# A GpSimd low part behind six norms, and the norm's inverse and spread ahead of the barrier

## The reference, cut to what matters

```
def rms_norm(x, g):
    xf = xf * lax.rsqrt(jnp.mean(xf * xf, axis=-1, keepdims=True) + RMS_EPS)
    return (xf * g.astype(jnp.float32)).astype(x.dtype)

h = modulate(rms_norm(x, norm_g[l, 1]), shift[:, 1], scale[:, 1])
x = x + gate[:, 1, None, :] * token_mixer(h, ...)
```

## Time and profile before

| what | value |
| --- | --- |
| median of 3 runs | 2968.79 us (2968.53 to 2969.40) |
| profiled execution, time | 2971.32 us |
| profiled execution, span | 2969.4 us |
| mean granted TensorE clock | 0.976 of full |
| TensorE matmul / weight load busy | 2870.5 (97%) / 2664.5 (90%) us |
| VectorE / ScalarE / GpSimd busy | 2183.7 (74%) / 1369.5 (46%) / 178.3 (6%) us |
| chain that ended last | TensorE 66%, VectorE 8%, weight load 4%, ScalarE 1% of the span |

### The profile page before, as it was taken

How to read it: one execution, slowest core, us unless ns; L and a number is a source line. 1 busy time by engine, 2 the same in 40 slices (tenths; PEclk the granted TensorE clock), 3 DMA queues, 4 the chain that set the end, 5 groups by cost and what they waited for, 6 DMA issues and landing times.

```text
span 2969.4 us, 61005 instructions
## 1 busy us (share of the span) xinstructions
PE 2870.5 (97%) x22452; PEld 2664.5 (90%) x22452; DVE 2183.7 (74%) x3774; ACT 1369.5 (46%) x2009; POOL 178.3 (6%) x189
## 2 busy tenths in 40 slices
PE   6999988989999999999999999999999999999999
PEld 6999976889999999999998888899999999988887
DVE  6777834457776668987779988756579877799765
ACT  3446532234444555554444445545555543444454
POOL 0112002200101000020000000000000200000000
PEclk9999986989999999999999999999999999999999
DMA  8885730038867454545445578653555444455554
GB/s 341 303 295 190 252 100 1 1 121 280 303 228 273 134 191 165 177 156 162 160 164 166 164 247 290 232 177 128 167 166 181 158 159 161 163 164 166 180 192 147
DMA packets 150621, 549.97 MB, mean 185 GB/s; under 512 B 16720, under 2 KB 16976, under 8 KB 150224
## 3 DMA queue, kind: packets, MB, share of 16 engines
q1 hardware_dynamic: 127584, 464.05, 46.6%
q0 software_dynamic: 22176, 80.75, 8.1%
q10 hardware_dynamic: 720, 3.17, 0.3%
HBM read 546.86 MB, written 1.05 MB: 185 GB/s over the span
## 4 chain that ended last, share of the span: by engine, by line
PE 66%; DVE 8%; PEld 4%; ACT 1%; issue 1%; PEldq 0%; POOLq 0%; POOL 0%; DVEq 0%; ACTq 0%
PE acc L2188 16%; PE st L1683 11%; PE st L1687 11%; PE st L1684 11%; PE acc L2195 8%; PE st L2154 3%; DVE w_lo L853 3%; DVE arena L1340 1%; PE acc L1687 1%; PE acc L1684 1%; PE acc L1683 1%; ACT w_hi L445 1%; DVE arena L893 1%; DVE arena L1375 1%; DVE arena L1345 1%
## 5 line engine op out<-in xcount | busy, mean ns | idle before, releaser
L853 DVE TENSOR_TENSOR w_lo<-ring,w_hi 128x1024 fp32r<-128x1024 f32 x860 | 1069.9, 1245 | 490.6 <-ACT w_hi L445 484.0
L445 ACT ACTIVATE w_hi<-ring 128x1024 fp32r<-128x1024 f32 x860 | 906.8, 1055 | 843.2 <-PE st L1687 764.5
L1683 PE MATMUL st<-h_hi,w_hi 128*128 128x256 f32 x4080 | 1016.6, 287 | 5.5 <-ACT arena L769 3.5
L1684 PE MATMUL st<-h_lo,w_hi 128*128 128x256 f32 x4080 | 1003.7, 283 | 0.0
L1683 PEld LDWEIGHTS st<-h_hi,w_hi 128*128 128x128 f32 x4080 | 784.3, 192 | 18.0 <-issue 11.5
L1684 PEld LDWEIGHTS st<-h_lo,w_hi 128*128 128x128 f32 x4080 | 785.0, 192 | 0.0
L1687 PE MATMUL st<-h_hi,w_lo 128*128 128x256 f32 x4080 | 577.2, 284 | 10.0 <-DVE w_lo L853 9.6
L1687 PEld LDWEIGHTS st<-h_hi,w_lo 128*128 128x128 f32 x4080 | 527.2, 192 | 15.7 <-DVE w_lo L853 15.4
L2188 PE MATMUL acc<-w_hi,act_hi 128*128 128x512 f32 x1016 | 319.5, 396 | 0.0
L2188 PE MATMUL acc<-w_hi,act_lo 128*128 128x512 f32 x1016 | 313.3, 390 | 0.0
L801 ACT ACTIVATE act_hi<-arena 128x256 fp32r (+1 forms) x256 | 106.8, 418 | 398.4 <-PE acc L2195 395.2
(11 more groups left out here) (314 smaller groups left out, 2797.7 us busy)
## 6 DMA issues: line engine op xcount, KB each, us to landing
ring<-weights SPq DMA_DIRECT2D x864, 512.0 KB, 3.3
arena<-ada_weights POOLq DMA_DIRECT2D x104, 512.0 KB, 5.1
extra<-ada_weights POOLq DMA_DIRECT2D x48, 512.0 KB, 4.5
arena<-ada_weights SPq DMA_DIRECT2D x16, 512.0 KB, 13.2
arena<-const ACTq DMA_DIRECT2D x1, 2112.0 KB, 11.8
x_t<-params SPq DMA_DIRECT2D x1, 1024.0 KB, 11.3
extra<-crows POOLq DMA_DIRECT2D x2, 512.0 KB, 4.5
out<-arena SPq DMA_DIRECT2D x4, 256.0 KB, 2.2
```

The lines of the kernel that those rows point to most:

```text
L445: nc_a.activation(w_hi[:, u % 2, :], ring[:, u % RING, :], ACT.Copy).then_inc(hi_ready, 1)
L853: v.tensor_tensor(w_lo[:, u % 2, :], ring[:, u % RING, :], w_hi[:, u % 2, :], ALU.subtract)\
L1683: mm(dst(t), w, hi_t(t), start=start, stop=False, skip_group_check=True)
L1684: mm(dst(t), w, lo_t(t), start=False, stop=False, skip_group_check=True)
```

## The change

Two things are moved. First, for norms 1, 2, 4, 5, 6 and 7, GpSimd makes the low part of the stage's second weight unit. It waits for that unit's high part, subtracts, and counts the new semaphore `second_lo`. VectorE, at the end of its `norm`, waits for that count and then writes one column of `spare` (128 x 1), whose completion counts `taken` as `lo(second)` did. Second, `inverted(n)` and `spread(n)` stand at the end of the stage before, ahead of the barrier, for norms 1 to 8; for norms 1 to 7 the four filler matmuls that followed the spread come behind the barrier. In `ffn(1)` the clearing of `acc` on TensorE stood ahead of the spread; now it stands behind it.

```diff
@@ VectorE
             def norm(n, a, b, dst, m=None, second=None):
-                if n > 0:
-                    inverted(n)
                 eng.wait_ge(sem("rstd"), n + 1)
...
                 if second is not None:
-                    lo(second)
+                    norm.seconds += 1
+                    eng.wait_ge(sem("second_lo"), norm.seconds)
+                    v.memset(spare[:, 1:2], 0.0).then_inc(taken, 1)
...
             ffn(0)
             scale1_of(1)
+            inverted(1)
             stage(eng, ST["ffn0"])
...
             lo(U_FFN2)
+            inverted(2)
             stage(eng, ST["mix_out"])
             ffn(1)
+            inverted(3)
             stage(eng, ST["ffn1"])
             norm(3, pc("final_g"), None, x_t)
             scale2_of(0, 0)
+            inverted(4)
             stage(eng, ST["final1"])
...
                 lo(U + O_WQ)
+                inverted(5 + 2 * l)
                 stage(eng, ST[f"out{l}"])
...
                     lo(U_L2 + N_L2)
+                inverted(6 + 2 * l)
                 stage(eng, ST[f"peer_d{l}"])
@@ GpSimd
+            def second(u):
+
+                eng.wait_ge(hi_ready, nth(u))
+                g.tensor_tensor(w_lo[:, u % 2, :], ring[:, u % RING, :], w_hi[:, u % 2, :], ALU.subtract)\
+                    .then_inc(sem("second_lo"), 1)
...
             stage(eng, ST["ffn0"])
+            second(U_MIX + 1)
             eng.wait_ge(sem("norm_lo"), 2 * DT)
...
                 stage(eng, ST[name])
+            second(U_FFN2 + 1)
             eng.dma_start(c_row, crows[1]).then_inc(sem("c_back"), 16)
             first_loads(8 * Q_C2)
...
             for l in range(LAYERS):
+                second(U_L2 + N_L2 * l + O_QK + 1)
                 if l == 0:
                     ada_loads(8 * Q_PROJ + ADA_RING, 8 * Q_WQ)
...
                 stage(eng, ST[f"out{l}"])
+                second(U_L2 + N_L2 * l + O_WQ + 1)
                 if l == 0:
                     ada_loads(8 * Q_WQ + ADA_RING, 8 * Q_LATE)
@@ TensorE
                 ins.then_inc(sem("rstd"), 1)
-                if 0 < n < 8:
-                    keep_busy(4)
...
-                if f == 1:
-                    spread(2)
                 first_two(base, [st[:, 0, 0:T], st[:, 2, 0:T]], rows_of((0, 2)[f]), False)
...
             ffn(0)
             squares(1)
+            spread(1)
             stage(eng, ST["ffn0"])
+            keep_busy(4)
...
-            spread(1)
             pairs(U_MIX, 26, "proj_out", 0, 1)
...
             squares(2)
+            spread(2)
             stage(eng, ST["mix_out"])
+            keep_busy(4)
             ffn(1)
             squares(3)
+            spread(3)
             stage(eng, ST["ffn1"])
-            spread(3)
+            keep_busy(4)
             squares(4)
+            spread(4)
             stage(eng, ST["final1"])
+            keep_busy(4)
             for l in range(LAYERS):
                 U = U_L2 + N_L2 * l
-                spread(4 + 2 * l)
...
                 squares(5 + 2 * l)
+                spread(5 + 2 * l)
                 stage(eng, ST[f"out{l}"])
-                spread(5 + 2 * l)
+                keep_busy(4)
...
                 squares(6 + 2 * l)
+                spread(6 + 2 * l)
                 stage(eng, ST[f"peer_d{l}"])
-            spread(8)
+                if l < LAYERS - 1:
+                    keep_busy(4)
```

More of the change, by code:

```diff
@@ L901, in norm @@
                 if second is not None:
-                    lo(second)
+                    norm.seconds += 1
+                    eng.wait_ge(sem("second_lo"), norm.seconds)
+                    v.memset(spare[:, 1:2], 0.0).then_inc(taken, 1)
+            norm.seconds = 0
             def dot(n, i=None, per=0):
```

## The result

The changed kernel takes 2990.18 us (median of 6 runs, 2988.27 to 2991.82) against 2968.66 for the kernel before beside it (median of 6, 2967.93 to 2976.71). The ratio is 1.0068, 95% interval 1.0055 to 1.0081: 20.2 us slower, 16.3 to 24.0. The forecast was 2980.5, with a range that ended at 2987. The direction was right, the size was a little over half. In a second session the same kernel took 2989.54, ratio 1.0055 (1.0038 to 1.0072), 16.4 us slower.

A forecast was written before the change was run, and what follows sets the result against it. VectorE's alternating norm chain, then TensorE's tail, then ScalarE's next unit were taken to set the path at the hand-overs. Losses of 8.3 + 1.4 + 2.1 - 0.1 = 11.7 us on 2968.79 gave 2980.5 us, range 2975 to 2987.

The forecast's parts named there:

- The hold: In norms with a second unit, VectorE's first low part stands still until GpSimd's tensor_tensor ends; 2.07 us at norms 1, 5, 6, 7.
- the sum: Over all norms: 8.3 (norms 1, 5, 6, 7), 1.4 (norm 2), 2.1 (norm 4), less 0.1 (norm 8), 11.7 us.
- The stall brings TensorE's clock down too: Rival: TensorE's idling in six norms lowers its clock, 0.9 us per norm, 5.4 in all, 2985.9 us; chance 0.10.
- clocks under 1.0 behind the stalls: Sign on TensorE's granted clock after each norm's stall: if it appeared, the prediction would be wrong.
- Norm 4's barrier: Barrier before norm 4 waits for GpSimd's queue; its 8.80 us were kept and moved 0.90 later, loss 2.1 us.
- `hi(second)` beside the norm: ScalarE's 1.06 us high part moves from beside inverse and spread to beside the norm; a loss near 0.2 us.
- Norm 2's gain from the moved clearing: In `ffn(1)`, clearing `acc` goes behind the barrier, where before it stood 1.03 us ahead of the spread.
- The 0.27 us of waiting for VectorE's low part: TensorE's wait in `first_two` at norm 1 for the second unit's low part; costs at most 0.06 us of path.
- The covers: In each norm, keep_busy(4) runs while ScalarE makes `hi(second)`, and the six memsets fall in VectorE's idle time; costed at nothing.
- No stall: Rival: the norm's L888 passes GpSimd's instruction by; +0.4 us in all, 2969.2 us, no change; chance 0.07.
- the cheaper hand-over: Rival: inverse and spread vanish from eight chains (1.03 each) and 0.27 at six is real; 9.8 less, 2959.0; chance 0.03.

The follow-up runs named there:

- e4_half: Changed kernel, but GpSimd makes 512 of the low part's 1024 columns and VectorE the rest at the norm's end: 2979.85 us, ratio 1.0025.
- e7_ahead: Changed kernel, but the second unit's high part (ScalarE) and low part (VectorE, not GpSimd) are made before the barrier: 2974.75 us, ratio 1.0005 to the kernel before.
- e2_gpsimd: Kernel before with only the second unit's low part given to GpSimd, inverse and spread still behind the barrier: 2984.84 us, ratio 1.0042.
- e3_filler: Changed kernel with 13 filler groups of two matmuls instead of 4 behind six barriers: 2985.31 us, ratio 1.0043 to the kernel before.
- e5_changed: The changed kernel timed again, unaltered, in a second session: 2989.54 us, ratio 1.0055 to the kernel before.
- e1_handover: Changed kernel with the low part back on VectorE, inverse and spread still ahead of the barrier: 2973.23 us, ratio 1.0002 to the kernel before.
- e6_loads: Changed kernel with GpSimd's four first loads issued behind norm 4's barrier instead of ahead of it: 2985.78 us, ratio 1.0043 to the kernel before.
- e10_before_loads: Kernel before with only GpSimd's weight loads issued behind norm 4's barrier instead of one barrier earlier: 2970.10 us, ratio 0.9994.
- e8_ahead_gpsimd: Changed kernel with the second unit's high part and GpSimd's low part both made ahead of the barrier: 2983.60 us, ratio 1.0033 to the kernel before.

## Why the prediction was half of the result

**The hold: right, in mechanism and in size.** Predicted: GpSimd 2381 ns, the held instruction ending 0.28 after it, the fourth norm row 2.07 later at norms 1, 5, 6 and 7 and 1.4 at norm 2. Measured: 2346 ns, 0.28, and 2.08, 2.00 at norms 5 to 7, 1.29 at norm 2. At norm 4 with the loads out of the way it is 2.08 (12.25 against 10.17). The hold with the hand-over makes 11.4 us over six norms, less 0.3 at norms 3 and 8, 11.1 against the 11.7 of the sum. e4_half ties it to GpSimd's duration one to one, e7_ahead shows it gone with the collision.

The rule of the Trainium skill quoted in the prediction (page "SBUF — State Buffer", section "Who interferes with whom") held at the meetings in these norms: the instruction with two SBUF inputs was held (L886 2.34 to 2.35 us). In the changed kernel the neighbouring L891 overlaps GpSimd's instruction by less than 0.1 us; that an instruction with its second input in PSUM isn't held is seen in e2_gpsimd, where two L893 at norm 1 lie wholly inside GpSimd's span and last 0.47. The other figure, 2.22 us as an estimate from the Trainium skill's "GPSIMD Engine Reference", section "Performance versus the Vector engine", was 0.13 low; the row of the trace before was 0.04 high.

**The clock: the step that failed.** "The stall brings TensorE's clock down too" had a chance of 0.10, with two reasons against it: the idle time would be shorter than the 2.74 us after which the clock had fallen before, and filler would run just ahead of it. The clock fell all the same: in the first profile behind 1.82 us of idle time at norms 1, 5 and 6 and behind 1.31 at norm 2, each with filler ahead, and in the second at norm 7 as well. At norm 4 it was low too, but there the barrier's wait of 4.43 us came first. The prediction had named clocks under 1.0 behind the stalls as a sign that it was wrong. Its price was nearly right: 0.9 a norm was forecast, 0.48, 0.55, 0.52, 0.74 and 1.78 measured at norms 1, 2, 4, 5 and 6 (norm 4 from the first norm row on: 11.36 against 10.84), 4.1 in all, against 5.4. Five matmuls took 1.06, not 1.2. The case that should have been the likeliest was put in the tail. e3_filler is what shows it: the same hold, TensorE idle for under 0.5 us, the clock at 1.00 at five norms, and 0.5 to 1.8 us less at those where it had fallen.

**Norm 4's barrier: a term taken as fixed.** The 8.80 us from barrier to barrier were moved along with the earlier barrier, to give 2.1. In the first profile the first norm row of norm 4 stood 5.71 us behind the square root, where before it was 3.87 and 3.9 followed from the prediction (872.50, less the square root at 868.76 less what norm 3 gains, 0.16): 1.8 us more. It is no constant: 4.11 in e3_filler, 4.31 in e5_changed, 5.54 in e1_handover and 6.29 in e4_half, and 1.40 in both changed kernels whose loads are moved. The loads are what is waited for: e6_loads and e10_before_loads show it, and in all nine traces with the loads ahead of this barrier GpSimd's drain ends 0.21 us behind the landing of the fourth load. That load took 6.7 us to land before and 8.6 in the changed kernel, which accounts for the 1.8. Why its landing differs, 6.7 to 9.2 us over the nine, stays open.

**The rest.** 11.1 + 4.1 + 1.8 make the 17 us of the norms. The range ended at 2987 because it was reached from one surprise at a time; clock and barrier both came, and 2980.5 + 4.1 + 1.8 is 2986.4 already. The measured 2990.2 lies 3.8 above that, which is about the 3 us that the norms don't show; what these are stays open. In the second session the same kernel was 16.4 slower, which on the median of the prediction is 2985.2. So whether the time falls into the range is in part chance; that the clock's term was missing from the sum is not.

**The small terms.** `hi(second)` beside the norm "a loss near 0.2": 0.12 to 0.18 in e1_handover, net of the earlier first row. Norm 2's gain from the moved clearing, about 0.5: 0.59. The 0.27 us of waiting for VectorE's low part, costed at 0.06 at most: with it gone, the third unit starts 1.37 us behind the second unit's low-weight matmuls (246.35 against 244.98), where it was 1.10. The wait just moved to ScalarE's third unit, and the removal of `lo(second)` gained nothing. The covers held: in the rows above neither keep_busy(4) nor a memset ends a wait.

**The rivals.** No stall, and the cheaper hand-over: both refuted, by the first trace and by e1_handover. e7_ahead has the cheapest hand-over of these kernels, 0.16 a norm, not 1.03: the drain behind the spread and the serial chain to the norm stay.

## What to carry to other kernels

Before giving work to GpSimd, look at what VectorE does in those microseconds: if its next instruction reads two SBUF tensors and is on the path, its wait is GpSimd's whole remaining time, and it matters little how small that instruction is by itself. A stall that is worked out for one engine must be followed into TensorE's clock: where the same trace shows the clock down after an idle time of like size, the low clock belongs in the sum, not in a rival. And a barrier that waited for a queue's loads is a term with a spread, not a number; it is cheap to ask whether those loads can be issued behind it.

## What was not expected of the hardware

The granted clock fell to 0.50 after TensorE had been idle for 1.82 us, behind 1.16 us of filler and two matmuls, and stayed there for 3 us at norm 1 but about 6 at norm 6; the same idle time left it at 1.00 at norm 7 in one execution and not in the other. Shorter idle times did it too: 1.31 us at norm 2, in both profiles of the changed kernel and in e6_loads, and 1.23 at norm 1 in e2_gpsimd, while 1.22 to 1.23 at norms 5 to 7 of that kernel did not. With GpSimd's instruction at 1.27 us TensorE idled for 0.74 at most in the hold, and the clock was low at norm 4 alone, where the barrier's long wait comes first. What decides between these cases no run here tells.

GpSimd's drain can end long after its last instruction: 3.4 us after a tensor_tensor at norm 1, 3.1 at norm 6, 0.1 at norms 2 and 7, all in one kernel (e8_ahead_gpsimd), with all loads landed long before. At norm 4 of the changed kernel the four load instructions are over in 2.08 us, and the barrier opens 10.4 us after their start (869.71 to 880.10), 0.2 us behind the landing of the last.

GpSimd's duration goes with its columns: 2.35 us for 1024, 1.27 for 512, fp32 in and fp32r out.
